# Prompt attention on one core: the scan's unused operand from a PSUM bank of its own, two banks for the transposes

## What is computed

```python
def _sb_block(q, k, v, q_pos, k_pos, bias):
    z = jnp.einsum('bqhd,bkhd->bhqk', q, k) * (SB_HEAD_DIM ** -0.5)
    z = z + bias[None, :, None, None]
    vis = k_pos[None, :] < q_pos[:, None]
    log_keep = jnp.where(vis, jax.nn.log_sigmoid(-z), 0.0)
    after = lax.cumsum(log_keep, axis=3, reverse=True) - log_keep
    a = jnp.where(vis, jnp.exp(jax.nn.log_sigmoid(z) + after), 0.0)
    return jnp.einsum('bhqk,bkhd->bqhd', a, v)
```

## Time and profile before

| | |
|---|---|
| median of 3 runs | 2846.69 us (2844.94 to 2848.82) |
| profiled execution, its own time | 2847.92 us |
| its span in the trace | 2846.1 us |
| prompt attention, in that span | 1737 to 2339.5 us, 602.5 us |
| granted TensorE clock, whole span | 0.942 of full speed |
| TensorE matmul busy, whole span | 2470.6 us (87%) |
| VectorE busy | 1235.7 us (43%) |
| ScalarE busy | 908.0 us (32%) |
| GpSimd busy | 935.8 us (33%) |
| costliest group on GpSimd | the multiplication L1599, 128 times, 445.4 us |
| costliest group on VectorE | the scan L1545, 128 times, 439.3 us |

### The profile page before, as it was taken

How to read it: one execution, slowest core, us unless ns; L and a number is a source line. 1 busy time by engine, 2 the same in 40 slices (tenths; PEclk the granted TensorE clock), 3 DMA queues, 4 the chain that set the end, 5 groups by cost and what they waited for, 6 DMA issues and landing times. The chain is left out here.

```text
span 2846.1 us, 37750 instructions
## 1 busy us (share of the span) xinstructions
PE 2470.6 (87%) x14209; PEld 1568.9 (55%) x14209; DVE 1235.7 (43%) x1625; ACT 908.0 (32%) x1746; POOL 935.8 (33%) x479
## 2 busy tenths in 40 slices
PE   5999899999499997899999874888888877886998
PEld 3555444444244443788888772555556555553443
DVE  1111056675300000555555424878687853441333
ACT  2222021232100001222223203878787852221110
POOL 2333010011000000544444203867786870003554
PEclk9999999999799998899999956999999988997999
DMA  5223211211222321111111018031220008994332
GB/s 149 98 92 100 45 38 46 62 32 45 54 57 42 80 90 49 39 30 44 31 43 42 18 36 195 16 65 34 57 48 16 16 14 304 324 318 166 130 130 84
DMA packets 161790, 233.32 MB, mean 82 GB/s; under 512 B 16496, under 2 KB 95361, under 8 KB 156568
## 3 DMA queue, kind: packets, MB, share of 16 engines
q1 hardware_dynamic: 161688, 231.93, 27.4%
HBM read 162.97 MB, written 68.91 MB: 81 GB/s over the span
## 5 line engine op out<-in xcount | busy, mean ns | idle before, releaser
L1599 POOL TENSOR_TENSOR f_a<-f_a,f_keep 128x144 f32<-128x144 f32 (+15 forms) x128 | 445.4, 3498 | 154.0 <-DVE f_keep L1545 154.0
L1545 DVE TENSOR_TENSOR_SCAN f_keep<-f_keep 128x144 f32<-128x144 f32 (+15 forms) x128 | 439.3, 3437 | 129.0 <-ACT f_a L1517 129.0
L614 PE MATMUL ps<-hT,wa 128*128 128x512 f32 (+1 forms) x960 | 353.6, 531 | 39.7 <-DMA wa<-w_in 39.0
L448 PE MATMUL ps<-hT,wc 128*128 128x512 f32 (+1 forms) x960 | 354.1, 531 | 12.3 <-DMA wc<-w_in 12.3
L614 PEld LDWEIGHTS ps<-hT,wa 128*128 128x128 f32 x960 | 168.3, 191 | 225.0 <-issue 225.0
L448 PEld LDWEIGHTS ps<-hT,wc 128*128 128x128 f32 x960 | 168.6, 191 | 197.0 <-issue 197.0
L1464 PE MATMUL ps<-con,f_a 128*128 128x128 f32 x1216 | 185.0, 294 | 70.6 <-POOL f_a L1599 69.3
L2012 PE MATMUL ps<-m_w,m_mT 128*128 128x512 f32 x544 | 238.0, 596 | 0.0
L322 PE MATMUL ps<-wt,hT_now 128*128 128x512 f32 x544 | 237.9, 595 | 0.0
L1443 PE MATMUL ps<-f_k,f_q 64*128 64x344 f32 (+19 forms) x832 | 186.2, 526 | 35.1 <-DMA f_k<-chan 34.6
L1464 PEld LDWEIGHTS ps<-con,f_a 128*128 128x128 f32 x1216 | 141.2, 149 | 109.8 <-POOL f_a L1599 87.3
(11 more groups left out here) (277 smaller groups left out, 3335.4 us busy)
## 6 DMA issues: line engine op xcount, KB each, us to landing
j_kp<-cache_k SPq DMA_DIRECT2D x128, 256.0 KB, 3.9
j_v<-cache_v SPq DMA_DIRECT2D x128, 256.0 KB, 4.7
chan<-y SPq DMA_DIRECT2D x12, 1088.0 KB, 6.0
chan<-ya SPq DMA_DIRECT2D x12, 1088.0 KB, 11.5
d_ld<-chan SPq DMA_DIRECT2D x16, 768.0 KB, 5.0
h_rows<-hg SPq DMA_DIRECT2D x17, 512.0 KB, 5.0
m_hh<-h_rows SPq DMA_DIRECT2D x17, 512.0 KB, 3.3
f_k<-chan SPq DMA_DIRECT2D x16, 516.0 KB, 14.5
```

Of the source, the lines that this page charges most:

```text
L448: m = pe.matmul(ps[:, ci, 0:n], wc[k][:, c, :], hT[:, c, c0:c0 + n], start=(c == 0), stop=(c == KC - 1))
L614: m = pe.matmul(ps[:, ci, 0:n], wc[k][:, c, :], hT[:, c, c0:c0 + n], start=(c == 0), stop=(c == KC - 1))
L1545: dve.tensor_tensor_scan(x, x, x, 1.0, ALU.mult, ALU.bypass).then_inc(scanned, 1)
L1599: pool.tensor_tensor(w, w, keep[i % KEEPS][:, L - n + 1:L + 1], ALU.mult).then_inc(weighed, 1)
```

## The change

The scan's second operand, which the bypass leaves without effect, is now one column of PSUM bank 6, broadcast over the width of the block; VectorE fills that column with 1.0 once, before the loop. So that bank 6 is free for it, the transposes get two banks (4 and 5) in place of three: group n goes to bank 4 + n % 2 and waits for the copy of group n - 2. The list `by_vector` and VectorE's copies, of which there were none, are taken out. On each engine the instructions stay the same and in the same order, but for the one memset.

```diff
+TURNS = 2
...
-    Z_BANK, T_BANK, O_BANK = 0, 4, 7
+    Z_BANK, T_BANK, IDLE_BANK, O_BANK = 0, 4, 6, 7
...
             def turn(i, g):
                 n, r = groups_to[i] + g, row_of(i)
                 if g == 0:
                     pe.wait_ge(weighed, START + i + 1)
-                if n >= 3:
-                    if by_vector[n - 3]:
-                        pe.wait_ge(out_dve, START + vector_to[n - 2])
-                    else:
-                        pe.wait_ge(out_act, START + scalar_to[n - 2])
+                if n >= TURNS:
+                    pe.wait_ge(out_act, START + n - TURNS + 1)
                 c = W - P * (r + 2)
                 for j in range(min(4, r + 2 - 4 * g)):
                     b = 4 * g + j
-                    m = pe.transpose(ps[:, T_BANK + n % 3, j * P:(j + 1) * P], a[i % RING][:, c + b * P:c + (b + 1) * P], p.ident)
+                    m = pe.transpose(ps[:, T_BANK + n % TURNS, j * P:(j + 1) * P], a[i % RING][:, c + b * P:c + (b + 1) * P], p.ident)
                 m.then_inc(turned, 1)
...
                 done = groups_to[i + 1] + g + 1
-                pe.wait_ge(out_dve, START + vector_to[done])
-                pe.wait_ge(out_act, START + scalar_to[done])
+                pe.wait_ge(out_act, START + done)
...
-                act.activation(at[i % 2][:, 512 * g:512 * g + nb], ps[:, T_BANK + n % 3, 0:nb], ACT.Copy).then_inc(out_act, 1)
+                act.activation(at[i % 2][:, 512 * g:512 * g + nb], ps[:, T_BANK + n % TURNS, 0:nb], ACT.Copy).then_inc(out_act, 1)
...
                 x = keep[i % KEEPS][:, L - n:L][:, ::-1]
-                dve.tensor_tensor_scan(x, x, x, 1.0, ALU.mult, ALU.bypass).then_inc(scanned, 1)
+                dve.tensor_tensor_scan(x, x, ps[:, IDLE_BANK, 0:1].broadcast_to([P, n]), 1.0, ALU.mult, ALU.bypass).then_inc(scanned, 1)
...
             for i in range(KEEPS):
                 x = dve.memset(keep[i][:, L:L + 1], 0.0)
+            x = dve.memset(ps[:, IDLE_BANK, 0:1], 1.0)
             x.then_inc(filled_v, 1)
```

More of the change, by code:

```diff
@@ L1346, in prompt_attention @@
     groups_to = np.cumsum([0] + groups).tolist()
-    by_vector = [False for n in range(groups_to[-1])]
-    vector_to = np.cumsum([0] + by_vector).tolist()
-    scalar_to = [n - v for n, v in enumerate(vector_to)]
     values_to = np.cumsum([0] + groups[1::2]).tolist()
@@ L1356, in prompt_attention @@
     mask_filled = p.sem("diagonal_filled")
-    turned, out_act, out_dve, av_done = p.sem("A_turned"), p.sem("AT_by_scalar"), p.sem("AT_by_vector"), p.sem("av_done")
+    turned, out_act, av_done = p.sem("A_turned"), p.sem("AT_by_scalar"), p.sem("av_done")
     gated, stored = p.sem("po_gated"), [p.sem(f"po{b}_stored") for b in range(2)]
     filled_v, filled_p, ready = p.sem("pa_filled"), p.sem("pa_padded"), p.sem("pa_bias_ready")
-    Z_BANK, T_BANK, O_BANK = 0, 4, 7
+    Z_BANK, T_BANK, IDLE_BANK, O_BANK = 0, 4, 6, 7
     with ExitStack() as st:
@@ L1520, in out @@
                 n = groups_to[i] + g
-                if by_vector[n]:
-                    return
                 nb = min(4, row_of(i) + 2 - 4 * g) * P
                 act.wait_ge(turned, START + n + 1)
-                act.activation(at[i % 2][:, 512 * g:512 * g + nb], ps[:, T_BANK + n % 3, 0:nb], ACT.Copy).then_inc(out_act, 1)
+                act.activation(at[i % 2][:, 512 * g:512 * g + nb], ps[:, T_BANK + n % TURNS, 0:nb], ACT.Copy).then_inc(out_act, 1)
             act.wait_ge(ready, START + 2)
@@ L1579, in _ @@
                 j = i - LAG
-                ng = groups[j] if 0 <= j < N else 0
-                for g in range(0, min(2, ng)):
-                    out(j, g)
                 if 1 <= i <= N:
@@ L1586, in _ @@
                     gate(j // 2 - 1)
-                for g in range(2, ng):
-                    out(j, g)
         @block.gpsimd
```

## The result

The changed kernel takes 2803.77 us in the median of 4 runs (2799.90 to 2808.73), against 2845.82 us before, in the runs taken together with it: a ratio of 0.9852, 95% interval 0.9834 to 0.9870. Forecast were 2800 us and a gain of 47; measured are 42, outside what a measurement of this kernel takes for no change.

A forecast was written before the change was run, and what follows sets the result against it. Scan and multiplication taking turns set the wide blocks' pace; afterwards ScalarE and TensorE would. Four sweeps saving 11.7 us each give 47, so 2847.92 - 47 = 2801, forecast 2800 us; range 2768 to 2832 for 8 in 10.

The forecast's parts named there:

- The mechanism: Wide blocks: VectorE's scan and GpSimd's multiplication hold each other; with one SBUF operand the scan runs beside the multiplication.
- The scan's price: Scan with a PSUM operand: no change taken from 2.09 ns a column; VectorE then off the path.
- The drawing of block 13: Block 13 (1808 columns), drawn from ScalarE and TensorE rows: 11.87 us with two banks, 11.36 with three; the trace has 13.20.
- The sum: Prompt attention: 9.5 us saved in blocks 8 to 15, 2.2 in block 0; 11.7 a sweep, 47 in four.
- the lost bank: Third transpose bank given up: 0.51 us in each of blocks 8 to 15, 16 us in all, inside the 47.
- The step: What the change adds: memset nothing, removed copy waits nothing; the real price is the third transpose bank.
- the hold's removal: Ending the time scans and multiplications hold each other in the prompt attention; 47 us saved after the bank's 16.
- More was won: Rival 1: ScalarE loses nothing in blocks 8 to 15 and block 0; four sweeps save 73 us, 2774; chance 0.14.
- That the change does not do what it says: Rival 2: VectorE still takes the operand's way from SBUF or holds it, hold stays; 2847 to 2853 us; chance 0.06.
- the third rival: Two banks make transposes and copies take turns, a bank's round 1.32 us, 2.8 a block; 2866 us; chance 0.06.

The follow-up runs named there:

- runs 1 and 2: Run 1: changed kernel with the scan's second operand in one SBUF column, 2849.0 us. Run 2: kernel before with two transpose banks, scan unchanged, 2847.4 us.
- run 3: Kernel before, three transpose banks and SBUF tile named twice, but the scan covers only 16 columns of each block: 2780.78 us, ratio 0.9769.
- the cut values: Changed kernel with a finished block's values split between the odd head's turn and the next turn: 2785.89 us, repeated at 2783.62 us.

## Why the prediction was right

**The mechanism, as predicted.** Scan and multiplication took turns on something that an operand in SBUF needs and one in PSUM does not. The gate product had said so before the change, and runs 1 and 2 show it: neither a single SBUF column nor the other parts of the change give any of the gain. The Trainium skill, "SBUF — State Buffer", section "Who interferes with whom", says that a VectorE instruction with two SBUF inputs contends with a GpSimd instruction that reads SBUF, and one with at most one, outside the 2-port perf modes, does not. The runs agree, and add that an operand counts even where the operation bypasses it, and where it is one repeated column (3.56 us for 144 columns).

**The scan's price, as predicted: none.** 4453 ns for 2064 columns, against 4.46 us where it was not held before. The fixed part that the Trainium skill's page "VectorE: DVE Perf Modes" gives to an instruction that reads PSUM, which by an estimate would have made 8 us of 128 scans, is not seen where only the second operand lies there: the shortest scan of 144 columns takes 427 ns, and took 425 before.

**The drawing of block 13: 11.87 us, measured 11.97; with three banks 11.36, measured 11.49.** The two waits that it leaves, 0.77 and 0.56 us, stand in the changed kernel's timeline of that block, 0.68 for the transposes behind the values and 0.48 for the scores behind the second group:

```profile
2250.27 1.09 PE L1459 MATMUL ps<-con,f_a 128*128 128x128 f32 x8
2250.97 1.08 ACT L1517 ACTIVATE f_at<-ps 128x512 f32<-128x512 f32 x2 [0.68 <-PE ps L1459]
2251.30 1.04 PE L1441 MATMUL ps<-f_k,f_q 64*128 64x456 f32 x4
...
2252.53 1.02 ACT L1510 ACTIVATE f_keep<-ps,f_bias 128x912 f32<-128x912 f32 x1 [0.48 <-PE ps L1447]
```

Before, the same place shows 0.56 and 0.48, and two more waits that led back to GpSimd. These are gone.

**The sum.** In the second sweep:

| blocks | before | forecast | measured | no hold, three banks |
|---|---|---|---|---|
| 0 | 12.10 | 9.9 | 11.69 | 8.88 |
| 1 | 9.26 | 9.26 | 8.73 | 7.87 |
| 2 to 7 | 31.39 | 31.39 | 31.38 | 31.39 |
| 8 to 15 | 94.93 | 85.4 | 86.12 | 82.73 |
| sum | 147.68 | 136.0 | 137.92 | 130.87 |

Blocks 8 to 15 save 8.8 us of the 9.5 forecast, blocks 2 to 7 nothing, as said. Block 0 depends on the sweep: 11.69 us at a granted clock of 0.85 in the second, 10.22 at 1.00 in the third and the fourth, near the 9.9 forecast; before it took 12.10, 12.09 and 10.94. So it saves 3.0 us in these three, and not 6.6. From the first gate to the last product the stage loses 600.34 - 557.23 = 43.1 us of the 47.

**What was mis-sized: the lost bank, and where it costs.** The step said that heads with at most two groups wait for no third bank, and that block 1 changes by nothing; it put the bank at 16 us, all in blocks 8 to 15. Measured are 23.6 us: 13.6 in blocks 8 to 15, 8 in blocks 0 and 1, some 2 at the end of the stage. While ScalarE begins the narrow heads of a new sweep, TensorE and the copies are still at the last heads of the old one, three turns behind, and these have four or five groups each. A narrow head has one piece of gates, so from its second pair of copies on no gates lie in between, and with two banks transposes and copies take turns. TensorE (PE) and ScalarE (ACT) in block 0 of the third sweep, first in the changed kernel, then in run 3 with three banks:

```profile
2015.43 1.09 PE L1459 MATMUL ps<-con,f_a 128*128 128x128 f32 x8
2016.12 1.09 ACT L1517 ACTIVATE f_at<-ps 128x512 f32<-128x512 f32 x2 [3.50 <-PE ps L1459]
2016.77 1.15 PE L1459 MATMUL ps<-con,f_a 128*128 128x128 f32 x8 [0.25 <-ACT f_at L1517]
2017.46 1.30 ACT L1517 ACTIVATE f_at<-ps 128x512 f32<-128x512 f32 x3 [0.26 <-PE ps L1459]
2018.11 0.33 PE L1459 MATMUL ps<-con,f_a 128*128 128x128 f32 x1 [0.20 <-ACT f_at L1517]
```

```profile
2007.07 2.16 PE L1459 MATMUL ps<-con,f_a 128*128 128x128 f32 x17
2007.76 2.23 ACT L1517 ACTIVATE f_at<-ps 128x512 f32<-128x512 f32 x5 [3.49 <-PE ps L1459]
```

A price by the width of the block being begun looks at the wrong head. On the other side the hold's removal was worth 66.5 us and not the 47 + 16 = 63 of the sum. The two errors nearly cancel: 3.5 more won, 7.6 more lost, and 47 became 43. That the total came out so close is in part luck.

**The rivals.** More was won (2774) is what a third bank or the cut values come near: 2781 and 2784 to 2786. That the change does not do what it says is refuted by the scans' times. Copies and transposes in turn did not come in the wide blocks, since the gates between two pairs of copies leave time for both transposes. They did come in blocks 0 and 1, where no gates lie between: a bank's round there is 2016.77 - 2015.43 = 1.34 us, and the third rival had 1.32. So its mechanism was right, and the sum left it out where its condition held. With one bank it came everywhere.

## What to carry to other kernels

An operand that an operation ignores is still read, and the memory it comes from can hold up another engine; where a VectorE instruction with two SBUF inputs, as this scan, and a long GpSimd instruction overlap in the timeline, look for durations that are the sum of two, and move one input to PSUM if a bank can be spared. Price the bank by the work that is in flight when it is short, with a pipeline's lag taken in, and not by the loop's current step. When two engines that feed each other become the bound, an uneven piece in one queue (here 3 us of values in every second turn) is what to split next: it took 17 to 18 us off the stage here.

## What was not expected

TensorE's granted clock rose with the hold's removal, from 0.95 of full speed in the stage to 0.98, though TensorE has the same work in less time. Among the runs here it goes with TensorE's idle time in the stage (from first gate to end, less its busy time): 0.83 with one bank, where TensorE is idle for 218 us; 0.94 to 0.95 with the hold, 88 to 95 us; 0.98 in the kernels without hold, 37 to 62 us. Before, the half-speed stretch at 2277.00, where eight transposes took 1.62 us and not 1.09, came after a wait of 2.33 us for GpSimd.

A wait alone does not decide it. Where the second and the third sweep of the changed kernel begin, TensorE waits 1.70 us for a copy both times, and only in the second do the eight transposes then take 1.84 us and not 1.14:

```profile
1872.25 1.84 PE L1459 MATMUL ps<-con,f_a 128*128 128x128 f32 x8 [1.70 <-ACT f_at L1517]
```

```profile
2010.17 1.14 PE L1459 MATMUL ps<-con,f_a 128*128 128x128 f32 x8 [1.70 <-ACT f_at L1517]
```

That block 0 ran at a granted clock of 0.85, the other at 1.00, and it took 1.47 us more. What decided is not shown. Nor was it separated how much of the 66.5 us is due to the clock and how much to the waits themselves; TensorE's busy time in the stage, 504.9 us before, is 490.5 in run 3.
